# The order of 16 attention units in the prompt stage of a one-layer hybrid decoder step

## What is computed

```
def nsa_attend(q, qpos, gates, kc, vc, ..., sel_k, sel_v, win_k, win_v, win_pos):
    p_c = masked_softmax(q . kc * scale, ...)        # 31 compressed keys
    o_c = p_c . vc
    ...
    p_s = masked_softmax(q . k_sel * scale, ...)     # selected blocks
    o_s = p_s . v_sel
    p_w = masked_softmax(q . win_k * scale, ...)     # sliding window
    o_w = p_w . win_v
    return gates[..., 0:1] * o_c + gates[..., 1:2] * o_s + gates[..., 2:3] * o_w
```

## Time and profile before

| | |
|---|---|
| median of 3 runs | 2091.45 us (2086.78 to 2093.21) |
| the profiled execution | 2081.51 us, its span 2079.8 us |
| prompt attention in the span | about 408 to 562 us |
| PE, DVE, ACT busy over the span | 86%, 71%, 53% |

### The profile page before, as it was taken

How to read it: one execution, slowest core, us unless ns; L and a number is a source line. 1 busy time by engine, 2 the same in 40 slices (tenths; PEclk the granted TensorE clock), 3 DMA queues, 4 the chain that set the end, 5 groups by cost and what they waited for, 6 DMA issues and landing times. The chain is left out here.

```text
span 2079.8 us, 27155 instructions
## 1 busy us (share of the span) xinstructions
PE 1783.8 (86%) x8975; PEld 1382.4 (66%) x8975; DVE 1466.6 (71%) x1413; ACT 1099.2 (53%) x1034; POOL 296.3 (14%) x327
## 2 busy tenths in 40 slices
PE   4999576787756398589999999999999999999981
PEld 3777464655534344478888888888888888888870
DVE  4421266355432245589999999999999999999983
ACT  3211333344321113167777777777777777777761
POOL 0000101110011140102121121212121212112110
PEclk9999877968978688599999999999999999999996
DMA  9253433230022440479999999999999999999963
GB/s 360 97 197 122 78 131 104 80 102 1 1 62 62 164 125 21 179 311 361 371 370 369 366 375 368 364 383 359 377 368 371 375 370 372 374 369 370 370 231 108
DMA packets 112151, 516.61 MB, mean 248 GB/s; under 512 B 25869, under 2 KB 47261, under 8 KB 59450
## 3 DMA queue, kind: packets, MB, share of 16 engines
q1 hardware_dynamic: 98666, 485.71, 62.5%
q0 software_dynamic: 13424, 30.12, 5.4%
HBM read 502.75 MB, written 31.81 MB: 257 GB/s over the span
## 5 line engine op out<-in xcount | busy, mean ns | idle before, releaser
L2221 PE MATMUL banks<-split 128*128 128x512 f32 x4608 | 1078.3, 393 | 1.6 <-DVE split L2365 1.6
L2221 PEld LDWEIGHTS banks<-split 128*128 128x128 f32 x4608 | 861.3, 189 | 194.2 <-issue 14.7
L2365 DVE TENSOR_TENSOR split<-expert_buffers,split 128x2048 fp32r<-128x2048 f32 x384 | 867.3, 2286 | 63.8 <-ACT split L2299 62.7
L2299 ACT ACTIVATE split<-expert_buffers 128x2048 fp32r<-128x2048 f32 x384 | 732.1, 1916 | 260.9 <-PE banks L2221 235.4
L2158 POOL TENSOR_TENSOR expert_buffers<-expert_buffers 128x1 f32<-128x1 f32 x63 | 61.0, 969 | 907.8 <-PE banks L2228 527.8
L444 PE MATMUL banks<-w_in_high,hT_high 128*128 128x476 f32 (+1 forms) x240 | 93.0, 387 | 7.7 <-DVE hT_low L370 7.7
L444 PE MATMUL banks<-w_in_low,hT_high 128*128 128x476 f32 (+1 forms) x240 | 91.3, 380 | 0.0
L444 PE MATMUL banks<-w_in_high,hT_low 128*128 128x476 f32 (+1 forms) x240 | 91.0, 379 | 0.0
L1784 PE MATMUL banks<-arena 128*128 128x512 f32 (+1 forms) x160 | 76.2, 639 | 14.4 <-DMA arena<-in_b_router 14.4
L383 DVE COPY arena<-banks 128x476 f32<-128x476 f32 (+1 forms) x15 | 9.8, 651 | 111.3 <-PE banks L444 111.3
L2369 DVE TENSOR_TENSOR split<-banks,split 128x1024 fp32r<-128x1024 f32 x64 | 77.8, 1215 | 0.0
(11 more groups left out here) (340 smaller groups left out, 1849.8 us busy)
## 6 DMA issues: line engine op xcount, KB each, us to landing
expert_buffers<-in_w_gate SPq DMA_DIRECT2D x128, 1024.0 KB, 7.7
expert_buffers<-in_w_up SPq DMA_DIRECT2D x128, 1024.0 KB, 6.6
expert_buffers<-in_w_down SPq DMA_DIRECT2D x128, 1024.0 KB, 9.1
arena<-in_w_ada SPq DMA_DIRECT2D x16, 1024.0 KB, 4.9
w_in_landing<-in_w_in SPq DMA_DIRECT2D x6, 1904.0 KB, 15.7
arena<-in_w_ada SPq DMA_DIRECT2D x4, 2048.0 KB, 19.1
arena<-in_x_prompt SPq DMA_DIRECT2D x8, 512.0 KB, 10.6
arena<-in_cache_cmp POOLq DMA_DIRECT2D x32, 128.0 KB, 3.3
```

What stands on the lines that cost most here:

```text
L2221: last = pe.matmul(ps[:, bank + c, :], x[:, kt * P:(kt + 1) * P].bitcast(F32R), wt.bitcast(F32R), start=False, stop=(kt == KT - 1 and x is ...
L2299: act.activation(high[:, j % RING_Q].bitcast(F32R), v, ACT.Copy).then_inc(s_high, 1)
L2365: dve.tensor_tensor(rest[:, j % RING_Q].bitcast(F32R), v, high[:, j % RING_Q], ALU.subtract).then_inc(s_rest, 1)
```

## The change

A function `tile_and_head(u)` takes the place of `divmod(u, GRP)` and `u // GRP` everywhere in the stage. The tile is now (3, 0, 2, 1)[u % 4] and the head group u // 4, so the units have 512, 128, 384, 256 keys, four times over. The hand-written order of the steps on each engine, the buffers and the semaphores stay as they are. Every unit does the same work as before; only the place of it in the sequence is another.

```diff
+    def tile_and_head(u):
+
+        return (3, 0, 2, 1)[u % (SEQ // P)], u // (SEQ // P)
+
     def keys_of(u):
-        return (u // GRP + 1) * P
+        return (tile_and_head(u)[0] + 1) * P
...
             def factors(u):
-                t, g = divmod(u, GRP)
+                t, g = tile_and_head(u)
...
             def finish(u):
-                t, g = divmod(u, GRP)
+                t, g = tile_and_head(u)
...
             def query(u, rows=slice(0, P)):
-                t, g = divmod(u, GRP)
+                t, g = tile_and_head(u)
...
             def score_cmp(u):
-                t = u // GRP
+                t = tile_and_head(u)[0]
...
-                    for kb in range(u // GRP + 1):
+                    for kb in range(tile_and_head(u)[0] + 1):
...
-                nb = u // GRP + 1
+                nb = tile_and_head(u)[0] + 1
```

## The result

The changed kernel takes 2099.23 us (median of 6 runs, 2098.12 to 2102.28), the kernel before 2087.85 in the 6 runs beside it (2085.12 to 2093.21). The ratio is 1.0053 with a 95% interval of [1.0038, 1.0068]: slower by 11.4 us. The forecast was 2099 and +7.6. That the time was met to the microsecond is luck: the median of before came down by 3.6, from 2091.45, once more runs were taken, and the step is larger than forecast by nearly as much.

The account below looks back on a forecast made before the run. A closed chain of PE, DVE and ACT waiting for each other was taken as the bound. Turns -1.5, late link +3.1, fill +4.5, tail -2.7 and clock +4.2 gave +7.6 us, so 2099 us, range +2 to +13.

Parts of the forecast that it names:

- the fill: Start of the stage up to scores(1, 1): a first unit of 512 keys instead of 128 costs 4.5 us more.
- the tail: Behind the last scores(15, 1): a last unit of 256 keys instead of 512 saves 2.7 us.
- the late link at full clock: Next-but-one unit's scores queue behind 512-key values on PE: 0.5 us lost each time, 1.6 at the first, 3.1 total.
- the late link at the lower clock: Scores behind 512-key values when the clock falls: 2.9 us each, two of four times 5.8, only 1.3 added.
- The chain as a rule: Full-clock turn between successive scores takes 5.63 + 0.91 a + 0.213 b us; a, b are next two units' 128-key blocks.
- Turns: The 14 turns from scores(1, 1) to scores(15, 1): smaller sums of a and b save 1.5 us.
- The clock: TensorE's lower clock over the 14 turns: costs 14.5 us after, between 4 and 24, against 10.3 before: +4.2.
- the rate: Clock loss of 0.94 us per turn, from seven turns of before, taken for all 14: 13.2 us.
- The second rival: Clock low behind every 512-key unit: 11.6 us on top of 13.2, clock term 24.8, kernel 2109 us; chance 0.17.
- The first rival: The mix of unit sizes holds TensorE's clock, its cost falls to 4 us, kernel 2088.5 us; chance 0.14.
- The third: Rival: the clock falls in each of the 14 turns at 2.36 us, kernel 2117 us; chance 0.03.
- The fourth: Rival: order does not matter, PE's late scores are hidden and clock costs 10.3 us again, kernel 2092 us; chance 0.10.

Follow-up runs that it names:

- filled order of before: Kernel before with eight unread products per unit put into PE's two waits: 2076.85 us, ratio 0.9927 to before.
- filled mix: Kernel before with units reordered to 512, 384, 128, 256 keys per head group and eight unread products per unit in PE's waits: 2077.01 us, ratio 0.9941 to before.
- early scores: Changed kernel with branch-0 scores of the next unit but one moved ahead of values(u) on PE: 2092.03 us, ratio 1.0018 to before.
- the other mix: Changed kernel with units reordered to 512, 384, 128, 256 keys per head group, no unread products added: 2083.95 us, ratio 0.9975 to before.
- the changed order: Where said with the fillers: changed kernel plus eight unread products per unit in PE's two waits, 2083.49 us, ratio 0.9971 to before.
- changed order with early scores and fillers: Changed kernel with branch-0 scores ahead of values(u) on PE and unread products in PE's waits: 2079.28 us, ratio 0.9939 to before.

## Why the prediction was right, and where it was not

The direction was right, the measured time lies in the stated range, and the chain, the fill, the tail and the late link at full clock came out near their forecasts. One term was booked far too small, the late link at the lower clock. That +11.4 still lies within +2 to +13 owes something to luck: the first pair of profiles, with the cost of before as the forecast had it, lies 16.4 apart.

**The chain as a rule** held. It was fitted on two turns, tested on one, and gave every later turn of the filled order of before to 0.1 us, and every one of the filled mix but (3, 1), 0.3 above. The turn (4, 1), 9.48 by the rule, was never seen at a clock of 1.00 without fillers; with early scores it took 9.58 to 9.68 at 0.98 and 0.99. One constant was too small: the first turn, which has no `back` and no `finish`, took 4.86 us at full clock in the filled order of before, 1.9 below the 6.75 of the rule, where I took off 1.1.

**Fill** was forecast at +4.5: the first `scores(1, 1)` came 422.83 - 411.76 = 11.07 us after the first scores, against 417.69 - 411.00 = 6.69 before. That is +4.4. **Tail**, forecast at -2.7, is -3.5 from `scores(15, 1)` to the next stage (579.83 - 566.31 = 13.52 against 562.66 - 545.65 = 17.01). **Turns**, -1.5 by the rule, were not measured by themselves for this order. For the filled mix the rule gives 2.0 less than for the filled order of before, and 0.6 was measured (117.08 - 116.52): the first turn of before, overestimated by the rule, and the turns (3, 1) take the rest.

**The late link** was forecast at 0.5 per turn (1, 3) at full clock, and took 0.61 (7.79 - 7.18). I had dropped its smaller form in the turns (2, 4), values of 384 keys ahead of scores of 512; it takes 0.17 at full clock, and the early scores took it away. The first turn, booked at 1.6, lost 0.74 (7.31 against 6.57 with early scores). So the sum at full clock, 0.74 + 1.8 + 0.5 = 3.0, met the 3.1 by two errors that cancel.

**The clock** is the term that was mis-sized. I forecast a cost of 14.5 us after, against 10.3 before. In after, turns of 143.48 and 142.1 stand 27.3 and 25.9 above the rule's 116.2; less 3.1 for the late link at full clock that is 23 to 24 us. In before, it is 10.3, 10.2 and 18.3 in three executions (turns less 117.7), 12.9 in the mean. Two steps failed. First, I took the late link at the lower clock for one in two of four turns, 5.8, and booked only 1.3 of it. In the trace of after the turns (1, 3) take 10.22, 10.42 and 8.28 in place of 7.18, and the turns (2, 4), which I did not count, take 11.19, 11.60 and 11.88 in place of 8.30. Those six turns alone hold 17.1 of the 27.3 us. Not all of it is the late link: with early scores DVE waits for scores in none of them, and (1, 3) still take 8.5 to 8.6 and (2, 4) 10.3. Over all 14 turns, moving the call took off 14.0 us (143.48 - 129.50) and the other mix 11.0 (143.48 - 132.00, less the rule's own 0.4). Without the 3.0 at full clock, the late link at the lower clock, with the share of the low clock that goes along with it, was worth 8 to 11 us in these profiles, where 1.3 was booked; by the medians of the early scores, 7 to 11 in all, it is 4 to 8. What stays above the rule without it, 13.3 and 16.3, is at or above the 13.2 that the rate gave. The second rival, which let the late link decide at the lower clock, gave 11.6 for it and 24.8 for the whole term. It is the mechanism that came true, at 23 to 24, though I had placed it in four turns and it sat in seven. Second, I read "the clock never falls in the last turns of 512 keys" out of one profile; in another execution of the same kernel one of these turns took 13.86 us at 10.13 by the rule. The loss of before by the clock is larger in the mean than in the profile shown, and this took back a part of the first error: +12.7 for the stage in place of +7.6.

The first rival, that the mix holds the clock, fell: 0.73 and 0.76 over the turns, under the 0.80 that was set as its sign. The third, a fall in every turn at 2.36 each, fell less far: two turns (3, 2) of after took 8.79 us, the rule to the digit, but each of the other 12 lost 0.46 or more. "At every second turn at most", which spoke against it, did not carry over from before to after. The fourth fell with the late link.

Not settled: why the clock falls where it does. With the fillers, the order of before and the mix 512, 384, 128, 256 held 1.00 throughout, while the changed order still fell in turns where a unit of 384 keys is followed by one of 256 or one of 512 by one of 128: in three of seven such turns, and in all seven with the scores early. The fillers don't cover the waits alike: those ahead of r = 2 start behind the exponentials of branch 1, and the wait that stays open ahead of them differs. It is at most 1.56 us in the two runs that held 1.00, but 1.83 to 1.99 in the turns (3, 2) and (4, 1) of the changed order. The longest such wait of the mix, in a turn (4, 3), and two of the changed order with early scores, (3, 2) and (4, 1):

```profile
453.36 0.94 PE L1328 MATMUL banks<-arena 128*128 128x128 f32 x6 [1.56 <-ACT arena L1135]
```

```profile
472.96 1.65 PE L1327 MATMUL banks<-arena 128*128 128x128 f32 x6 [1.83 <-ACT arena L1135]
...
492.40 0.94 PE L1327 MATMUL banks<-arena 128*128 128x128 f32 x6 [1.98 <-ACT arena L1135]
```

The clock fell only in turns with these longer waits, but in four of seven of them without early scores it held. So the open wait goes with the fall and does not decide it alone. No run filled it too.

## What to carry to other kernels

Write the chain of a pipelined turn as a sum of links in the sizes of the units it touches. If every link is of one unit's size, a mix of sizes gains nothing. Then ask of each queue what now stands ahead of a small unit's next step: an engine with slack at equal sizes (here PE with the values of the unit before) becomes a link where a large unit's leftovers meet a small unit's short turn, and weighs more when its clock is low (3.39 us for 1.97 here). And where one profile shows a clock that varies, take a second one of the same kernel before a term is sized from it.

## What the runs showed of the hardware that I had not expected

The same program has a different cost of the clock from one execution to the next: the 14 turns of before took 127.96, 127.95 and 136.04 us, at mean clocks of 0.80, 0.80 and 0.72, with nothing changed. And 128 products without use, put where PE waits, made the kernel 12.6 us faster (0.9927 [0.9903, 0.9951]), since they held the clock at 1.00 for 117 us. Where the clock was low all the same, five such products took 2.26 us at a mean clock of 0.55, where they take 1.28 at full clock (timeline of the changed order with early scores and fillers, at 494.71), ahead of the transposes that the turn waits for:

```profile
494.71 2.26 PE L1327 MATMUL banks<-arena 128*128 128x128 f32 x10
...
496.81 0.60 PE L1283 MATMUL banks<-arena 128*128 128x128 f32 x4
...
497.34 0.49 PE L1262 MATMUL banks<-arena 64*128 64x128 f32 x4
```

The trace counts each product twice, so its ten are five.
